# Products over 528 tokens, cut 256 + 272 in place of 264 + 264

## The reference: two layers over 528 tokens

```
h = concat(meta_tokens, x)                      # 528 x 1024
for layer in (0, 1):
    h = h + 0.5 * swiglu(rmsnorm(h), ff1)       # 1024 -> 2 x 2816 -> 1024
    if layer == 0:                              # gated convolution and state-space model
        z = rmsnorm(h) @ w_in                   # 1024 -> 2048
        h = h + concat(conv(z), ssm(z)) @ w_out # the ssm ends in a product with glu_w, 512 -> 512
    else:                                       # window attention
        h = h[:, 16:] + attention(rmsnorm(h)) @ w_o
    h = h + 0.5 * swiglu(rmsnorm(h), ff2)
return h
```

## Time and profile before

| | before |
|---|---|
| median of three runs | 1881.71 us |
| the profiled execution | 1882.0 us |
| its span | 1880.0 us |
| TensorE matmuls busy | 1865.3 us, 99%, 13887 |
| TensorE weight loads busy | 1765.6 us, 94%, 13887 |
| VectorE busy | 955.1 us, 51%, 1077 |
| ScalarE busy | 599.6 us, 32%, 707 |
| GpSimd busy | 350.8 us, 19%, 629 |
| mean granted TensorE clock | 0.998 |

### The profile page before, as it was taken

The page is one execution under the profiler, slowest core; times in us unless marked ns, Lnnn a source line. Parts: engine busy times, 40 slices in busy tenths (PEclk is TensorE's granted clock), DMA queues, the critical chain, the costliest instruction groups (busy, mean ns, idle before and its releaser), DMA issues.

```text
span 1880.0 us, 33855 instructions
## 1 busy us (share of the span) xinstructions
PE 1865.3 (99%) x13887; PEld 1765.6 (94%) x13887; DVE 955.1 (51%) x1077; ACT 599.6 (32%) x707; POOL 350.8 (19%) x629
## 2 busy tenths in 40 slices
PE   8999999999999999999999999999999999999999
PEld 8999999999999999999999999999988788888887
DVE  5444356568765443344564443445556654434443
ACT  5222222332243222222342222223456442222232
POOL 2888889414330000000000000000012000000000
PEclk9999999999999999999999999999999999999999
DMA  7332444547523332433243323322321233333423
GB/s 183 90 84 84 142 147 128 163 126 185 137 69 90 90 84 84 120 82 83 70 126 90 84 84 101 90 81 71 112 73 46 62 96 92 92 94 104 110 70 87
DMA packets 330785, 188.29 MB, mean 100 GB/s; under 512 B 8152, under 2 KB 323832, under 8 KB 330712
## 3 DMA queue, kind: packets, MB, share of 16 engines
q1 hardware_dynamic: 323296, 166.81, 32.0%
q0 software_dynamic: 7088, 20.38, 4.0%
q10 hardware_dynamic: 328, 0.07, 0.0%
HBM read 174.91 MB, written 11.14 MB: 99 GB/s over the span
## 4 chain that ended last, share of the span: by engine, by line
PE 95%; DVE 2%; issue 1%; ACT 1%; DMA 1%; ACTq 0%; POOL 0%; SPq 0%; DVEq 0%
PE ps L799 78%; PE ps L1015 5%; PE ps L1057 2%; PE ps L1126 2%; PE ps L1076 1%; PE ps L1265 1%; PE ps L1227 1%; DMA raw<-in_ff_w_down 1%; PE ps L844 1%; PE ps L1167 0%; PE ps L976 0%; PE ps L975 0%; PE ps L966 0%; DVE r L1592 0%; DVE wl L1563 0%
## 5 line engine op out<-in xcount | busy, mean ns | idle before, releaser
L799 PE MATMUL ps<-xh,wh 128*128 128x264 f32 (+1 forms) x2432 | 557.7, 299 | 0.3 <-DVE t_a L1616 0.2
L799 PE MATMUL ps<-xh,wl 128*128 128x264 f32 (+1 forms) x2432 | 556.6, 298 | 0.0
L799 PE MATMUL ps<-xl,wh 128*128 128x264 f32 (+1 forms) x2432 | 556.6, 298 | 0.0
L1563 DVE TENSOR_TENSOR wl<-raw,wh 128x2048 fp32r<-128x2048 f32 x171 | 398.3, 2329 | 173.6 <-ACT wh L1276 173.6
L1276 ACT ACTIVATE wh<-raw 128x2048 fp32r<-128x2048 f32 x172 | 327.5, 1904 | 248.6 <-PE ps L799 205.7
L799 PEld LDWEIGHTS ps<-xh,wh 128*128 128x128 f32 x2432 | 384.9, 188 | 15.3 <-issue 1.4
L799 PEld LDWEIGHTS ps<-xl,wh 128*128 128x128 f32 x2432 | 384.8, 188 | 13.8 <-issue 0.2
L799 PEld LDWEIGHTS ps<-xh,wl 128*128 128x128 f32 x2432 | 384.8, 188 | 13.8
L799 PE MATMUL ps<-act_h,wh 128*128 128x264 f32 (+1 forms) x1232 | 282.2, 298 | 1.2 <-DVE wl L1563 1.2
L799 PE MATMUL ps<-act_h,wl 128*128 128x264 f32 (+1 forms) x1232 | 281.6, 298 | 0.0
L799 PE MATMUL ps<-act_l,wh 128*128 128x264 f32 (+1 forms) x1232 | 281.5, 298 | 0.0
(11 more groups left out here) (308 smaller groups left out, 1681.3 us busy)
## 6 DMA issues: line engine op xcount, KB each, us to landing
raw<-in_ff_w_gate SPq DMA_DIRECT2D x88, 512.0 KB, 4.0
raw<-in_ff_w_up SPq DMA_DIRECT2D x87, 512.0 KB, 5.2
raw<-in_ff_w_down SPq DMA_DIRECT2D x64, 384.0 KB, 4.0
raw<-in_ff_w_down SPq DMA_DIRECT2D x64, 320.0 KB, 3.7
raw<-in_even_w_in SPq DMA_DIRECT2D x16, 512.0 KB, 5.3
raw<-in_attn_w_qkv SPq DMA_DIRECT2D x12, 512.0 KB, 4.4
raw<-in_even_w_out SPq DMA_DIRECT2D x8, 512.0 KB, 4.5
raw<-in_attn_w_o SPq DMA_DIRECT2D x8, 512.0 KB, 4.6
```

The source lines that it names most:

```text
L799: last = nc.tensor.matmul(ps[:, 2 * pair + hf, 0:nh], w[:, slot, b * P:(b + 1) * P], x[:, k0 + k, c0 + hf * nh:c0 + (hf + 1) * nh], start= ...
L1563: v.tensor_tensor(wl[:, c % 2, :], raw[:, c % 2, :], wh[:, c % 2, :].bitcast(F32), ALU.subtract).then_inc(wl_ready, 1)
```

## The change

The pieces of `ALL` become 256 and 272 columns. The first is written to the second half of its bank (columns 256 to 511), the second to the start of the next (columns 0 to 271), so that the 528 results of a pair lie one behind the other across the border of the two banks, and the readers take them as one run of 528. The triples lose their third number. The layout in SBUF, the order of the instructions, the waits and the buffers stay as they are; the single-bank products of 512 columns too.

```diff
-    ALL = (0, L // 2, 2)
-    REAL = (META, SEQ, 1)
-    FRONT = (0, SEQ, 1)
+    ALL = (0, L)
+    HALF = SEQ // 2
+    REAL = (META, SEQ)
+    FRONT = (0, SEQ)
...
+        flat = ps[:].rearrange("p b n -> p (b n)")
...
         def span(col):
-            c0, nh, nb = col
-            return slice(c0, c0 + nb * nh)
+            return slice(col[0], col[0] + col[1])
+
+        def pieces(col):
+
+            c0, n = col
+            return [(512 - HALF, c0, HALF), (512, c0 + HALF, n - HALF)] if n > 512 else [(0, c0, n)]
...
-        def halves(ap, col):
-
-            return ap[:, span(col)].rearrange("p (b n) -> p b n", b=col[2]) if col[2] > 1 else ap[:, span(col)]
-
         def banks(b, col):
-            return ps[:, b:b + col[2], 0:col[1]] if col[2] > 1 else ps[:, b, 0:col[1]]
+
+            at = b * 512 + pieces(col)[0][0]
+            return flat[:, at:at + col[1]]
...
                     for q, (w, x) in enumerate(((wh, x_h), (wh, x_l), (wl, x_h))):
-                        for hf in range(nb):
-                            last = nc.tensor.matmul(ps[:, 2 * pair + hf, 0:nh], w[:, slot, b * P:(b + 1) * P],
-                                                    x[:, k0 + k, c0 + hf * nh:c0 + (hf + 1) * nh],
+                        for at, x0, nh in pieces(col):
+                            last = nc.tensor.matmul(flat[:, 1024 * pair + at:1024 * pair + at + nh], w[:, slot, b * P:(b + 1) * P],
+                                                    x[:, k0 + k, x0:x0 + nh],
                                                     start=(k == 0 and q == 0), stop=(k == n - 1 and q == 2))
...
-            v.tensor_scalar(halves(sq, col), banks(4, col), 1.0 / DM, EPS, ALU.mult, ALU.add).then_inc(var_ready, 1)
+            v.tensor_scalar(sq[:, span(col)], banks(4, col), 1.0 / DM, EPS, ALU.mult, ALU.add).then_inc(var_ready, 1)
...
-                hd = halves(h[:, d, :], col)
+                hd = h[:, d, span(col)]
...
-                            v.tensor_tensor(halves(t_a, col), tile(0, col), halves(r, col), ALU.mult).then_inc(tile_evac, 1)
+                            v.tensor_tensor(t_a[:, span(col)], tile(0, col), r[:, span(col)], ALU.mult).then_inc(tile_evac, 1)
...
-                    v.tensor_tensor(u_t.rearrange("p (t b c) -> p b c t", t=T, b=2), tile(p % 2, ALL).rearrange("p b (c t) -> p b c t", t=T),
-                                    halves(r, ALL).rearrange("p b (c t) -> p b c t", t=T), ALU.mult).then_inc(tile_evac, 1)
+                    v.tensor_tensor(u_t.rearrange("p (t c) -> p c t", t=T), tile(p % 2, ALL).rearrange("p (c t) -> p c t", t=T),
+                                    r[:, span(ALL)].rearrange("p (c t) -> p c t", t=T), ALU.mult).then_inc(tile_evac, 1)
```

More of the change, by code:

```diff
@@ L804, in token_sums @@
             def token_sums(m, col):
-                c0, nh, nb = col
                 pe.wait_ge(ssq_step, (KD + 1) * m)
-                for hf in range(nb):
-                    last = nc.tensor.matmul(ps[:, 4 + hf, 0:nh], ones[:], ssq[:, c0 + hf * nh:c0 + (hf + 1) * nh], start=True, stop=True)
+                for at, x0, nh in pieces(col):
+                    last = nc.tensor.matmul(flat[:, 2048 + at:2048 + at + nh], ones[:], ssq[:, x0:x0 + nh], start=True, stop=True)
                 last.then_inc(ssum_full, 1)
@@ L842, in first_job @@
                             pe.wait_ge(gate_split[1], 1 if k == 0 else 2)
-                        for hf in range(nb):
-                            last = nc.tensor.matmul(ps[:, hf, 0:nh], w[:, 0, k * P:(k + 1) * P], x[:, k, c0 + hf * nh:c0 + (hf + 1) * nh],
+                        for at, x0, nh in pieces(col):
+                            last = nc.tensor.matmul(flat[:, at:at + nh], w[:, 0, k * P:(k + 1) * P], x[:, k, x0:x0 + nh],
                                                     start=(k == 0 and q == 0), stop=(k == KD - 1 and q == 2))
@@ L857, in second_job @@
                             pe.wait_ge(wl_ready, 1)
-                        for hf in range(nb):
-                            last = nc.tensor.matmul(ps[:, 2 + hf, 0:nh], w[:, 0, (KD + k) * P:(KD + k + 1) * P], x[:, k, c0 + hf * nh:c0 + (hf + 1) * nh],
+                        for at, x0, nh in pieces(col):
+                            last = nc.tensor.matmul(flat[:, 1024 + at:1024 + at + nh], w[:, 0, (KD + k) * P:(KD + k + 1) * P], x[:, k, x0:x0 + nh],
                                                     start=(k == 0 and q == 0), stop=(k == KD - 1 and q == 2))
@@ L1013, in _ @@
                     for q, (w, x) in enumerate(((wh, xh), (wh, xl), (wl, xh))):
-                        for hf in range(2):
-                            last = nc.tensor.matmul(ps[:, 2 * (p % 2) + hf, 0:L // 2], w[:, slot, b * P:(b + 1) * P], x[:, k, hf * L // 2:(hf + 1) * L // 2],
+                        for at, x0, nh in pieces(ALL):
+                            last = nc.tensor.matmul(flat[:, 1024 * (p % 2) + at:1024 * (p % 2) + at + nh], w[:, slot, b * P:(b + 1) * P], x[:, k, x0:x0 + nh],
                                                     start=(k == 0 and q == 0), stop=(k == KD - 1 and q == 2))
@@ L1027, in glu_blocks @@
                     for q, (w, x) in enumerate(((wh, act_h), (wh, act_l), (wl, act_h))):
-                        for hf in range(2):
-                            last = nc.tensor.matmul(ps[:, 2 * (j % 2) + hf, 0:L // 2], w[:, GLU[0] % 2, b * P:(b + 1) * P], x[:, 2 * KC + k, hf * L // 2:(hf + 1) * L // 2],
+                        for at, x0, nh in pieces(ALL):
+                            last = nc.tensor.matmul(flat[:, 1024 * (j % 2) + at:1024 * (j % 2) + at + nh], w[:, GLU[0] % 2, b * P:(b + 1) * P], x[:, 2 * KC + k, x0:x0 + nh],
                                                     start=(k == 0 and q == 0), stop=(k == KC - 1 and q == 2))
@@ L1055, in _ @@
                     for q, (w, x) in enumerate(((wh, act_h), (wh, act_l), (wl, act_h))):
-                        for hf in range(2):
-                            last = nc.tensor.matmul(ps[:, 2 * (d % 2) + hf, 0:L // 2], w[:, slot, b * P:(b + 1) * P], x[:, k, hf * L // 2:(hf + 1) * L // 2],
+                        for at, x0, nh in pieces(ALL):
+                            last = nc.tensor.matmul(flat[:, 1024 * (d % 2) + at:1024 * (d % 2) + at + nh], w[:, slot, b * P:(b + 1) * P], x[:, k, x0:x0 + nh],
                                                     start=(k == 0 and q == 0), stop=(k == KD - 1 and q == 2))
@@ L1121, in query_part @@
                             pe.wait_ge(hn_var, g)
-                c0, width, _ = REAL
+                c0, width = REAL
                 for k in range(half * KD // 2, (half + 1) * KD // 2):
@@ L1212, in out_part @@
             def out_part(d, k0, k1, sums=None):
-                c0, width, _ = FRONT
+                c0, width = FRONT
                 if k0 == 0:
@@ L1429, in _ @@
                 act.wait_ge(tile_full, GLU[1] + k + 1)
-                nc.scalar.activation(halves(t_b, ALL), banks(2 * (k % 2), ALL), ACT.Sigmoid,
+                nc.scalar.activation(t_b[:, span(ALL)], banks(2 * (k % 2), ALL), ACT.Sigmoid,
                                      bias=vec[:, V_GLUB + k:V_GLUB + k + 1]).then_inc(tile_evac, 1)
@@ L1615, in gate_up @@
                             dve.wait_ge(tile_full, j + 1)
-                            v.tensor_tensor(halves(t_a, col), tile(0, col), halves(r, col), ALU.mult).then_inc(tile_evac, 1)
+                            v.tensor_tensor(t_a[:, span(col)], tile(0, col), r[:, span(col)], ALU.mult).then_inc(tile_evac, 1)
                             dve.wait_ge(tile_full, j + 2)
                             wait(dve, act_ready[n], k)
-                            v.tensor_tensor(halves(t_c, col), tile(1, col), halves(r, col), ALU.mult).then_inc(tile_evac, 1)
+                            v.tensor_tensor(t_c[:, span(col)], tile(1, col), r[:, span(col)], ALU.mult).then_inc(tile_evac, 1)
                             dve.wait_ge(tile_evac, j + 2)
@@ L1750, in evac @@
                     wait(dve, u_out, 16 * i)
-                    v.tensor_tensor(u_t.rearrange("p (t b c) -> p b c t", t=T, b=2), tile(p % 2, ALL).rearrange("p b (c t) -> p b c t", t=T),
-                                    halves(r, ALL).rearrange("p b (c t) -> p b c t", t=T), ALU.mult).then_inc(tile_evac, 1)
+                    v.tensor_tensor(u_t.rearrange("p (t c) -> p c t", t=T), tile(p % 2, ALL).rearrange("p (c t) -> p c t", t=T),
+                                    r[:, span(ALL)].rearrange("p (c t) -> p c t", t=T), ALU.mult).then_inc(tile_evac, 1)
                 else:
-                    v.tensor_tensor(halves(dst, ALL), tile(p % 2, ALL), halves(r, ALL), ALU.mult).then_inc(tile_evac, 1)
+                    v.tensor_tensor(dst[:, span(ALL)], tile(p % 2, ALL), r[:, span(ALL)], ALU.mult).then_inc(tile_evac, 1)
             def conv(i):
```

## The result

The changed kernel takes 1902.55 us (median of four runs, 1901.05 to 1903.58), the kernel before 1882.07 us in the same comparison. The ratio is 1.0111 with an interval of 1.0098 to 1.0124: the change costs 20 us. I had forecast 1847 us.

The account below looks back on a forecast made before the run. TensorE, busy 99%, was taken as the bound: matmul count by interval. From 1882.0 us, 35.7 saved on pairs and 1 lost to waits gave 1847.3, put at 1847 us, range 1841 to 1884.

Parts of the forecast that it names:

- The pair: Two matmuls covering 528 columns: 35 units of 6.67 ns (16 columns at 2.4 GHz) for 36, saving 35.7 us.
- the counts: Matmuls of 264 columns: 10752, making 5376 pairs, of which 5360 run at full clock; none added or removed.
- both ends set for it: Bounds on the change per pair of matmuls: between -6.7 and +3.3 ns, with -6.7 taken.
- A piece costs its blocks of 64 bytes, half blocks counted whole: Matmul interval: 64-byte blocks covered plus 1 unit; 264 columns cover 17 blocks, 256 cover 16, giving 113.3 ns for 256.
- An aligned start saves: Operand reads: starting 64 bytes off was seen to cost; the second piece moves from byte 1056, mid-block, to byte 1024.
- Linear cost, no change: Rival: a pair depends on its 528 columns alone, stays at 240.0 ns, 1882 us; chance 0.24.
- Only the start counts: Rival: only the second piece's start matters, 2.5 ns by 5360 is 13.4 us, 1869 us; chance 0.12.
- The load sets the pace: Rival: the weight load holds 256-column pieces at 120.0 ns, 272-column pieces cost 3.3 ns more, 1900 us; chance 0.13.
- Evacuation: VectorE and ScalarE reading one run of 528 in place of two of 264: hidden, taken as 0, at most 1.6 us.
- The half clock: First 21 us at 1.2 GHz: about 15 pairs take 0.44 us each and lose nothing beside their columns.
- The waits: TensorE's waits on other engines, 11.3 us together before; they must stay near 12 us.
- The microsecond for crowding: Weight loads crowded by table loads at 350 to 360 us, and state-input round trips in the mixer: 1 us lost for both.

Follow-up runs that it names:

- e2: Not a kernel: 45 stretches of 60 matmul pairs, varying sizes, starts and PSUM place; 264+264 took 240.0 ns a pair, 256+272 244.0.
- e7: Not a kernel: 78 stretches of 50 pairs, seven cuts of 528 columns with shifted operand starts; the 56 combinations took 240.0 to 250.0 ns a pair.
- e6: Not a kernel: 47 stretches of 60 pairs with smaller sizes, fewer weight columns and shifted operands; 224+224 took 223.3 ns a pair, 256+256 240.0.
- e5: Changed kernel (256+272) with both weight buffers starting 64 bytes later: 1889.86 us, ratio 1.0046.
- e8: Kernel before (264+264) with its weights starting 128 bytes later: 1918.87 us, ratio 1.0202.
- e9: Kernel before (264+264) with weights and moving operands both starting 128 bytes later: 1881.54 us, ratio 0.9999.
- e1: Changed kernel, keeping its PSUM placement, with the pieces cut to 264 and 264 columns again: 1881.32 us, ratio 0.9998.

## Why the prediction was wrong

The step that failed is "The pair": 35 units of 6.67 ns in place of 36. Measured are 36.6 (244.0 / 6.67). The bound, the counts and the way from a pair to the kernel were right: 5360 pairs by the measured 4.0 ns give the profiled execution's growth to 0.2 us, and that of the medians to 0.9 us. The term had the wrong sign, and +4.0 ns lies outside both ends set for it (-6.7 and +3.3). Two premises of it fell.

- *A piece costs its blocks of 64 bytes, half blocks counted whole.* This explained 120.0 ns for 264 columns with one number and foretold 113.3 for 256. Two pieces of 256 take 240.0 ns (e2) at the place where they lie, 233.3 with x 8 columns on (e7), 226.7 with 64 weight columns (e6). The interval isn't a property of the size. I had taken two sizes, 264 and 512, both at one place, for a law over sizes.
- *An aligned start saves.* The rows from which I took this (226.7, 229.2 and 233.5 ns) did not show alignment but distance, which is where the moving operand starts measured from where the weights start: with both 64 bytes off, 512 columns take 226.7 again (e5, e7). Nor did the aligned start save in the pair. The second piece of the kernel before starts 32 bytes behind a multiple of 256, that of the new cut on one, and 264+264 with the second start at column 256 costs 246.7.

What stands in its place: a pair takes its 528 columns (220.0 ns) and a loss. Counted in the forecast's unit of 6.67 ns, 264+264 loses 3.0 on average, 256+272 loses 3.6 (18 in five pairs), 272+256 loses 4.0. The unit is a way of counting; no trace shows one such loss by itself. The loss goes with the sizes and with the distance between the two operands' starts, taken modulo 256 bytes. e5, e8 and e9 show this in the kernels, the table of e7 in stretches.

These two don't fix it wholly. The rows of 264+264 with the second start at column 256 and with both at column 0 have the same sizes and the same starts modulo 256 bytes. The first takes 246.7 ns (e2, and again in e6), the second 242.7 (e2, e6) and, run again in e6, 240.0.

Both operands are read at once, one for the stream and one for the next load (loads are busy for 1786.5 of the 1901.6 us). That these reads hinder one another is the reading that fits, not a thing that a run has shown directly.

The Trainium skill speaks against that reading ("TensorE: Matmul & The Clock Gate", section "Step-by-step: what each phase is for"): the two operands have read ports of their own, and "Loading the next tile's weights doesn't steal SBUF read bandwidth from the running matmul." Here moving the weights by 64 bytes turned 244 ns into 240, and by 128 bytes 240 into 246.7. For these products the measurement decides: where the weights lie does change the interval of the stream. Whether by read bandwidth or by something else that the two share, no run tells.

Of the rivals:

- *Linear cost, no change* (1882 us): wrong. Ten cuts of the same 528 columns take from 240.0 to 286.7 ns. The form of law for which I had named the Trainium skill's section "Back-to-back issue gap" falls with it for these products. That section gives it for a matmul by itself, and says that in a stream of loads and matmuls both set the spacing; I had left that out.
- *Only the start counts* (1869 us): wrong in the sign, and in that a start counts against the weights' and not by itself.
- *The load sets the pace* (1900 us): nearest in time, 2.6 us off, and partly right in mechanism. The 256-column pieces did win nothing, as two of them at 240.0 ns show. But not because a load needs 120 ns: 224+224 and 240+240 columns run at 111.7 and 112.0 each. And the same 256 and 272 columns run at 240.0 with the weights moved, which a pace set by the load's length excludes. It gave 243.3 for the pair, and 244.0 was measured; I would not call it the cause.

The smaller steps held. Evacuation: priced at 0, measured 707 against 708 ns and 1881.32 us in e1. The 512-column rows kept 226.7 ns. The half clock: 0.44 us, no loss. The waits: 11.7 us against 11.3. The microsecond for crowding wasn't tested, since TensorE came later and not earlier.

Left open: what the loss is inside the chip; and why one and the same stretch can fall into two or three patterns (264+264 with starts alike modulo 256 bytes: 246.7, 242.7 and 240.0 ns; 264+264 at distances 8 and 32; 256+272 with both operands by 32; e8's two feed-forwards). The state in which a stretch begins may choose, but no run took that apart.

## What to carry to other kernels

- An interval read at one size and one pair of addresses is a figure for these alone. Before you change how a product is cut, or move a buffer, measure the new sizes at the very distance (modulo 256 bytes) between moving operand and weights. Stretches of 50 or 60 pairs foretold the kernels to within some 0.2 ns a pair. Repeat each one: where a repeat gave a second value (246.7 and 244.4 ns at distance 32), the kernel showed both (e8).
- Round numbers are no merit: 264+264 was already at the lowest value found for 528 columns, and 256+272 was not.
- Where results lie in PSUM was free here (264+264 takes 240.0 ns with its first piece at column 0 or 248 of the bank, 256+272 takes 244.0 ns at 0 or 256, both in e2), across a bank border too, so that choice can follow the readers.

## What the runs showed that was not expected

- The start of the weights, by itself, is worth 37 us in 1882 (e8), and 0 if the other operand moves along (e9).
- 256+256 and 264+264 columns take the same 240.0 ns; from 240+240 (224.0) to 256+256 it is 0.5 ns for each of the 32 columns added, where the clock gives 0.42, and the 16 after that cost nothing.
- With 96, 64 or 32 weight columns, 512-column products are slower (230.0, 230.0, 231.7 ns) than with 128 (226.7).
